# State-space stage: the samples' B and C rows in two row groups of the array, spread by matmuls that alternate between them

## What is computed

```
xs, bm, cm = jnp.split(xbc_act, [SSD_D_INNER, SSD_D_INNER + g * n], axis=-1)
xdt = (xs * dt[..., None])
h_last = h0 * exp(dt * a)[..., None] + xdt (x) bm        # per sample, head, p, n
y      = sum over n of cm * h_last
```

## Time and profile before

| | |
|---|---|
| median of 3 runs | 1839.0 us (1838.51 to 1839.18) |
| profiled execution, its own time | 1834.96 us |
| span of the profiled execution | 1833.4 us |
| mean granted TensorE clock | 0.907 of full speed |
| TensorE busy (matmuls) | 88% of the span |
| VectorE busy | 41% of the span |

### The profile page before, as it was taken

One profiled execution on the slowest core, in us unless ns is written; L12 is line 12 of the kernel. 1 busy time (PEld: TensorE's weight loads), 2 busy tenths in 40 slices (PEclk: granted clock), 3 DMA queues, 4 the chain that ended last, 5 costly groups with the idle time before them and its releaser, 6 DMA issues. The chain is left out here.

```text
span 1833.4 us, 22894 instructions
## 1 busy us (share of the span) xinstructions
PE 1605.6 (88%) x8053; PEld 1234.2 (67%) x8053; DVE 759.3 (41%) x1821; ACT 504.2 (28%) x919; POOL 108.2 (6%) x147
## 2 busy tenths in 40 slices
PE   6989999998987998989999999996675888888686
PEld 3877787777765786878768767765353655566375
DVE  3057776776676102001541460451652333344313
ACT  3133233323331100021331332332441233333102
POOL 0011112111210000000010001001000000000000
PEclk7989999999997997998997997996786999999888
DMA  5075435543460340242052015004005544442111
GB/s 174 3 208 164 141 93 164 161 143 92 135 192 26 105 124 1 70 104 69 1 117 57 24 44 130 23 0 133 6 1 160 143 134 120 116 116 70 47 56 47
DMA packets 141544, 170.20 MB, mean 93 GB/s; under 512 B 46532, under 2 KB 108348, under 8 KB 141132
## 3 DMA queue, kind: packets, MB, share of 16 engines
q1 hardware_dynamic: 130120, 129.38, 24.4%
q0 software_dynamic: 11344, 39.79, 7.9%
HBM read 149.20 MB, written 24.32 MB: 95 GB/s over the span
## 5 line engine op out<-in xcount | busy, mean ns | idle before, releaser
L273 PE MATMUL psum<-arena 128*128 128x260 f32 x1536 | 356.2, 390 | 7.4 <-DMA arena<-in_ssd_w_in 7.4
L1484 PE MATMUL psum<-arena 128*128 128x260 f32 x1408 | 335.3, 396 | 7.8 <-DMA arena<-in_nsa_w_in 5.4
L273 PEld LDWEIGHTS psum<-arena 128*128 128x128 f32 x1536 | 291.8, 192 | 60.4 <-DMA arena<-in_ssd_w_in 7.8
L1484 PEld LDWEIGHTS psum<-arena 128*128 128x128 f32 x1408 | 271.2, 196 | 64.4 <-issue 12.5
L326 PE MATMUL psum<-arena 128*128 128x128 f32 (+9 forms) x1367 | 198.2, 289 | 96.5 <-DVE arena L1763 24.0
L326 PEld LDWEIGHTS psum<-arena 128*128 128x128 f32 (+9 forms) x1367 | 154.3, 148 | 148.3 <-issue 57.9
L1053 PE MATMUL psum<-arena 128*128 128x260 f32 x656 | 149.4, 390 | 8.8 <-PEq L593 6.9
L1053 PEld LDWEIGHTS psum<-arena 128*128 128x128 f32 x656 | 127.0, 194 | 31.0 <-issue 9.6
L1190 PE MATMUL psum<-arena 128*128 128x252 f32 x512 | 123.8, 404 | 5.4 <-ACT arena L1185 5.4
L1190 PEld LDWEIGHTS psum<-arena 128*128 128x128 f32 x512 | 103.7, 205 | 22.3 <-issue 4.8
L1688 ACT ACTIVATE arena<-arena 128x128 f32<-128x128 f32 (+3 forms) x128 | 71.9, 562 | 131.6 <-DVE arena L1780 126.8
(11 more groups left out here) (261 smaller groups left out, 1740.1 us busy)
## 6 DMA issues: line engine op xcount, KB each, us to landing
arena<-in_cache_kv SPq DMA_DIRECT2D x128, 256.0 KB, 4.1
arena<-in_ssd_w_in SPq DMA_DIRECT2D x16, 1024.0 KB, 5.4
arena<-in_nsa_w_in SPq DMA_DIRECT2D x16, 1024.0 KB, 5.2
arena<-scr_rows POOLq DMA_DIRECT2D x16, 520.0 KB
arena<-in_ssd_w_in SPq DMA_DIRECT2D x16, 512.0 KB
arena<-scr_rows POOLq DMA_DIRECT2D x8, 1024.0 KB, 6.5
arena<-in_state_ssm POOLq DMA_DIRECT2D x16, 512.0 KB, 6.9
out_ssm_sample<-arena POOLq DMA_DIRECT2D x16, 512.0 KB, 7.0
```

The source lines that it names most:

```text
L273: mm = nc.tensor.matmul(psum[:, b + h, 0:HALF], w[:, k, n % 2 * P:(n % 2 + 1) * P], xn[:, k, h * HALF:(h + 1) * HALF], start=(k == 0), sto ...
L1484: mm = nc.tensor.matmul(psum[:, pair + h, 0:HALF], w[:, k, at * P:(at + 1) * P], xn[:, k, h * HALF:(h + 1) * HALF], start=(k == 0), stop=( ...
```

## The change

The constant `samp` holds the 0/1 matrices of the 8 samples. Before, all lie in partitions 0 to 7. Now those of samples 0, 1, 4 and 5 lie in partitions 0 to 7, and those of samples 2, 3, 6 and 7 in partitions 64 to 71, at half the columns. The B and C rows are made twice, in partitions 0 to 7 and 64 to 71, by four plain matmuls against the identity where two transposes stood; ScalarE's copy covers 72 partitions where it covered 8. The four spreading matmuls go through the samples in the order 0, 2, 1, 3 (and 4, 6, 5, 7) where it was 0, 1, 2, 3, so that each has another 32 rows of the array and another PSUM bank than the one before it. Each sample's rows land where they landed before. The number of semaphores, waits, DMAs and the work of VectorE and GpSimd are the same.

```
-    put("samp", np.repeat(np.eye(NB), P, 1))
+    samp = np.zeros((64 + NB, 4, P), np.float32)
+    for b in range(NB):
+        samp[64 * (b // 2 % 2) + b, b // 4 * 2 + b % 2] = 1
+    put("samp", samp.reshape(64 + NB, 4 * P))
...
-                tr(psum[0:NB, 6, 0:P], act_[:, 2, SEQ:T], P)
-                tr(psum[0:NB, 6, P:256], act_[:, 3, SEQ:T], P).then_inc(sbc_full.sem, 1)
+                for q in range(2):
+                    for k in range(2):
+                        mm = nc.tensor.matmul(psum[64 * k:64 * k + NB, 6, q * P:(q + 1) * P], act_[:, 2 + q, SEQ:T], ident,
+                                              start=True, stop=True)
+                mm.then_inc(sbc_full.sem, 1)
...
-                    for b in range(4):
-                        mm = nc.tensor.matmul(psum[:, 4 + b // 2, (b % 2) * 256:(b % 2) * 256 + 256],
-                                              const("samp", NB)[:, (4 * r + b) * P:(4 * r + b + 1) * P], bcs[0:NB, :],
-                                              start=True, stop=True)
+                    for e in range(2):
+                        for k in range(2):
+                            mm = nc.tensor.matmul(psum[:, 4 + k, e * 256:(e + 1) * 256],
+                                                  const("samp")[64 * k:64 * k + NB, (2 * r + e) * P:(2 * r + e + 1) * P],
+                                                  bcs[64 * k:64 * k + NB, :], start=True, stop=True)
...
-                nc.scalar.activation(bcs[0:NB, :], psum[0:NB, 6, 0:256], ACT.Copy).then_inc(sbc_out.sem, 1)
+                nc.scalar.activation(bcs[0:64 + NB, :], psum[0:64 + NB, 6, 0:256], ACT.Copy).then_inc(sbc_out.sem, 1)
```

## The result

Median before 1838.4 us (20 runs, 1826.6 to 1846.2), after 1845.2 us (20 runs, 1836.1 to 1852.7): ratio 1.0038, 95% interval 1.0022 to 1.0054. By the medians the change makes the kernel 6.8 us slower. Executions of one kernel lie up to 12 us to either side of its median, and the profiled execution of the change is a long one (1852.6 us, that of before 1835.0). So the two profiles are compared stage by stage and not by their spans: the state-space stage, for one, starts 2.2 us later in the profile after, where the wait for a load of weights ahead of it was longer.

What follows compares the result with a forecast made beforehand. It took the stage to run at VectorE's pace from the first spread to L743, otherwise at TensorE's. Terms -7.65 + 1.4 + 10.1 gave +3.8 us, hence 1842.8 us; range 1832.0 to 1846.5.

Steps and rivals of the forecast that it cites:

- A spread of 1.07 us: State-space stage: a paired spread holds TensorE for 1.07 us where it took 1.92, priced from L1577.
- First spread 0.85 in eight turns: VectorE starts 0.85 us earlier in each of eight turns, and all up to L743 with it: 6.8 us gained.
- Second spread of the last turn, 0.85 more: In turn 7 VectorE waits for the second spread, so pairing it gains 0.85 us more.
- Doubled rows, 0.39 each, 1.4 in all: Four plain matmuls replacing two transposes cost 0.39 us more, partly hidden before L721 in odd turns; 1.4 us together.
- The rival by which they cost 0.82: Doubled rows cost 0.82 us more and the clock falls as forecast: 1846.1 us, slower, chance 0.07.
- A longer wait, 2.56 us, 2.25 in turn 0: TensorE's wait before L743 grows from 1.71 to 2.56 us in six turns, and to 2.25 in turn 0.
- The clock falls in six of seven turns, 1.68 each, 10.1 us: TensorE's clock falls to half behind the wait before L743 in turns 1 to 6, costing 1.68 us each, 10.1 together.
- What the falls give back, taken as 0: The stage's two existing hidden clock falls, in turns 2 and 6, give nothing back if they go.
- The sum: Spread gain and row cost, -6.3 us, plus clock falls, +10.1, make the kernel 3.8 us slower.
- the sum without the clock: Gain of 7.65 us from the spreads less 1.4 us for the doubled rows: -6.3 us.

Runs made afterwards that it cites:

- the filled wait: The changed kernel with five extra matmuls, which nothing reads, put into TensorE's wait before L743 in turns 0 to 6; ratio 1.0007 to before.
- the piece moved: The projection piece between L743's two halves put ahead of the first half; ratio to before 0.9937 in the kernel before, 0.9903 in the changed kernel.
- the first spread alone: The changed kernel with the second spread put back to partitions 0 to 7, doubled rows kept; ratio 0.9995 to before.
- the second spread alone: The changed kernel with the first spread put back to partitions 0 to 7, doubled rows kept; ratio 1.0077 to before.
- less work: The kernel before with two third-projection matmuls left out of the 48 records ahead of the wait, turns 0 to 6; ratio 1.0061 to before.

## Why the prediction was right, point by point

- **A spread of 1.07 us**: measured 193.14 - 192.07 = 1.07. L1577, the nearest row, gave the price exactly.
- **First spread 0.85 in eight turns**: L965 has no idle before it, and odd turns gain 0.83 to 0.86. Right.
- **Second spread of the last turn, 0.85 more**: wrong here. In the first profile turn 7 gains 0.92 in all, what its first spread gives. Its second spread comes behind a wait of 2.01 us and ran, this time, at a granted clock of 0.53; it holds TensorE for 576.14 - 574.20 = 1.94 us, and VectorE waits 0.92 for it as before. The price was taken at full clock, which this place doesn't always have: in the second profile of the change, at 1.00, the same spread holds TensorE for 572.66 - 571.59 = 1.07 us, and L709 to L743 takes 24.36 us where it took 25.38; but the wait before L743 is then 3.41 us, half clock follows, and L743 to L761 takes 12.19 us.
- **Doubled rows, 0.39 each, 1.4 in all**: they hold TensorE for 187.03 - 186.49 = 0.54 us where the transposes took 0.21, so 0.33; with the next piece, 0.10 longer in this record of it, some 0.4. Alone they cost 1.8 us up to L743, hidden in odd turns as forecast, 0.3 to 0.4 in turns 2, 4 and 6 and 0.76 in turn 0, where the clock also fell in the 48 records (12.48 us) and the fall outlasted the wait. In the change the even turns lose 0.35 to 0.38 against the odd, and turn 0 0.5. Slightly under-sized. The rival by which they cost 0.82 falls. In turn 0 before, twelve transposes (L326, twelve records of 128 columns) hold TensorE for 113.22 - 111.91 = 1.31 us and six plain matmuls (L721, twelve such records) for 128.03 - 126.59 = 1.44 us, so a transpose was about twice as fast here. The Trainium skill, in "TensorE: Matmul & The Clock Gate" (Terms), has four times for fp32; this trace doesn't agree.
- **A longer wait, 2.56 us, 2.25 in turn 0**: measured 2.57 in six turns and 2.23.
- **The clock falls in six of seven turns, 1.68 each, 10.1 us**: the mechanism is shown by the filled wait and by the piece moved. The number was seven, turn 0's 2.23 us with them, in both profiles of the change; each cost 1.49 to 1.69, 11.3 in all. The two waits of 2.28 and 2.39 us that kept the clock misled me on turn 0. They do not always keep it: ahead of the same transposes the second profile of before has half clock behind a wait of 2.22 us, and over all eleven profiles 11 of 22 such waits (1.99 to 2.39 us) were followed by it.
- **What the falls give back, taken as 0**: in the first profile turn 7's half clock behind L743 is gone (10.94 to 9.30, 1.64 us back); it stands ahead of L743 now, in the second spread and the piece behind it. This is not an effect of the change alone: the second profile of before takes 9.31 us there too. Not foreseen.
- **The sum**: forecast -6.3 + 10.1 = +3.8. Measured in the stage: -5.2 + 11.3 - 1.6 + 0.8 = +5.2; timed +6.8. Direction and mechanism hold. The falls were mis-sized by 1.2 us and the sum without the clock by 1.1; the -1.6 and +0.8 were not in it, nor was the loss outside the stage told of next. That the sum comes out so near is in part luck, since these errors have both signs.

**What stays open.** Outside the stage the changed kernel loses some 2.3 us more, which with the stage's 5.2 makes 7.5 beside the timed 6.8. In the attention layer, from the first L1591 to the last L1484, all four profiled kernels that have the transposes take 343.2 to 343.4 us, and all seven with the doubled rows 345.5 to 345.8. In these the clock falls once more; the piece of 32 records there, before and then after:

```profile
1150.50 7.29 PE L1484 MATMUL psum<-arena 128*128 128x260 f32 x32
```

```profile
1157.33 8.97 PE L1491 MATMUL psum<-arena 128*128 128x260 f32 x32
```

The code of that layer is the same. Two waits for a DMA ahead of it, both at one line (L1524, now L1531), are some 0.3 to 0.4 us longer (4.21 and 3.76 us before, 4.51 and 4.19 after). What in the change reaches so far was not tried; the loss goes with the doubled rows, or with what else these seven kernels share, and not with the falls in the state-space stage. With it the change would have gained some 3 us without any fall (-5.2 + 2.3), and not 6.3. These 2.3 us are also a part of the 4 and 6 us by which the times of the first spread alone and of the filled wait miss their expected -5; the rest is not placed. Both profiles of the change are of long executions (1852.6 and 1852.1 us, mean granted clock 0.899, where the median of its 20 is 1845.2 us and 0.902), so it isn't shown that the median execution has seven falls.

## What to carry to other kernels

When a shorter piece of work makes an engine only arrive earlier at a wait, look at what the clock did behind waits of the new length, and price a fall where it would stand: behind the wait it is on the path, ahead of it it is hidden. Let independent work follow the engine to that wait (here one piece moved past two lines) before shortening what stands ahead; the same edit then gained 13.6 us of the stage in the profiles, and 6.3 us timed, where it had cost 5.2 and 6.8. Price each repetition at the clock of its own place: the last turn's spread ran at half clock in one profile and at full in the next. And don't take what followed a wait in one profile for what always follows it: the waits of over 2 us that kept the clock here were followed by half clock in other profiles.

## What the runs showed of the hardware that was not expected

- Idle time of 2.2 to 2.6 us between dense matmuls was followed by half clock in 14 of 14 turns in two profiles of the change, but in 4 of 7 and 3 of 6 with the same waits in the kernels with the second spread alone and with less work. Wait length alone doesn't decide it; what else does was not found. In turn 7 a wait of 3.41 us was followed by half clock in the second profile of the change, and by full clock with the second spread alone, where L751 takes its usual 1.10 us:

```profile
589.35 1.10 PE L751 MATMUL psum<-arena 128*64 128x128 f32 x16 [3.41 <-DVE arena L990]
```

- The clock also fell with no wait longer than 0.26 us just ahead. Behind spreads of 1.92 us, with 8 rows in use at a time, the 48 records took 12.48 us in turns 2 and 6 before and in turn 1 with the first spread alone. In the profile of the piece moved without the change, where there is no wait left to hide them, the three falls that I found, in turns 0, 2 and 4, made L709 to L743 0.8 to 1.1 us longer there than in odd turns (30.68, 30.94 and 30.86 against 29.88); in the one with paired spreads there were none up to L743 in turns 0 to 6.
- Doing less can cost more: 0.88 us of work less per turn, 11 us slower, of which 4.8 us are seen right behind the longer waits.
